# Separate gate and up weights in the FFN, and an earlier split of the latent key weights, in a two-layer float32 trunk

## What is computed

```python
def layer_norm(x, g, b):
    ...
    y = (xf - mu) * lax.rsqrt(var + LN_EPS) * g + b

def swiglu(h, w_gate, w_up, w_down):
    return (jax.nn.silu(h @ w_gate) * (h @ w_up)) @ w_down

def mla_project(h, pos, w_dq, g_q, w_uq, w_dkv, g_kv, w_uk):
    c_q = rms_norm(h @ w_dq, g_q)          # w_dq: 1024 x 512
    ...
    kv = h @ w_dkv                         # w_dkv: 1024 x 320
    ...

for i in range(DEPTH):                     # 0: pool mixer, 1: latent attention
    ...
    hp = layer_norm(ALPHA * hp + mix_p, ln_g[i, 0], ln_b[i, 0])
    hp = layer_norm(ALPHA * hp + swiglu(hp, ffn_w_gate[i], ffn_w_up[i], ffn_w_down[i]), ln_g[i, 1], ln_b[i, 1])
    # and the same for the sample rows hs
```

## Time and profile before

| | us |
|---|---|
| median of 3 runs | 2572.41 |
| lowest, highest | 2571.08, 2573.94 |
| profiled execution | 2571.08 |
| its span, first to last instruction | 2569.3 |

### The profile page before, as it was taken

The page is one execution under the profiler, slowest core; times in us unless marked ns, Lnnn a source line. Parts: engine busy times, 40 slices in busy tenths (PEclk is TensorE's granted clock), DMA queues, the critical chain, the costliest instruction groups (busy, mean ns, idle before and its releaser), DMA issues.

```text
span 2569.3 us, 35922 instructions
## 1 busy us (share of the span) xinstructions
PE 2463.7 (96%) x13347; PEld 2120.0 (83%) x13347; DVE 1080.4 (42%) x1967; ACT 544.8 (21%) x945; POOL 639.3 (25%) x388
## 2 busy tenths in 40 slices
PE   8899999999999969999999999978999999999996
PEld 8799999999999858577777774448999999999995
DVE  4343444344434562434444454432344434443446
ACT  3311111111111253233223223433111111111112
POOL 3422222222222430111111100242222222222225
PEclk9999999999999989999999999989999999999998
DMA  5201111111111020100000003411111111111111
GB/s 174 58 25 49 49 38 35 49 49 39 35 49 49 29 61 16 36 16 17 17 17 17 9 9 100 148 49 50 49 49 34 39 49 49 35 38 49 49 33 70
DMA packets 132443, 117.84 MB, mean 46 GB/s; under 512 B 8896, under 2 KB 119448, under 8 KB 132352
## 3 DMA queue, kind: packets, MB, share of 16 engines
q1 hardware_dynamic: 132368, 116.83, 14.7%
HBM read 110.94 MB, written 6.42 MB: 46 GB/s over the span
## 4 chain that ended last, share of the span: by engine, by line
PE 92%; DVE 4%; issue 2%; ACT 1%; POOL 0%; DMA 0%; SPq 0%; ACTq 0%; DVEq 0%
PE ps L647 22%; PE ps L646 22%; PE ps L648 21%; PE ps L926 4%; PE ps L992 3%; PE ps L896 2%; PE ps L979 1%; PE ps L868 1%; PE ps L910 1%; PE ps L1076 1%; PE ps L901 1%; PE ps L716 1%; PE ps L1051 1%; PE ps L942 1%; PE ps L664 1%
## 5 line engine op out<-in xcount | busy, mean ns | idle before, releaser
L646 PE MATMUL ps<-XH,WGH 128*128 128x368 f32 x2112 | 699.4, 331 | 17.6 <-POOL WGL L1794 13.6
L647 PE MATMUL ps<-XL,WGH 128*128 128x368 f32 x2112 | 699.6, 331 | 0.0
L648 PE MATMUL ps<-XH,WGL 128*128 128x368 f32 x2112 | 697.1, 330 | 0.0
L1551 DVE TENSOR_TENSOR XR<-XR,ps 128x512 f32<-128x512 f32 x756 | 510.3, 685 | 8.8 <-PE ps L648 4.5
L1534 DVE TENSOR_TENSOR HF<-SG,ps 128x368 f32<-128x368 f32 x132 | 70.9, 537 | 939.9 <-PE ps L648 934.1
L646 PEld LDWEIGHTS ps<-XH,WGH 128*128 128x128 f32 x2112 | 398.5, 189 | 22.3 <-issue 18.9
L647 PEld LDWEIGHTS ps<-XL,WGH 128*128 128x128 f32 x2112 | 397.8, 188 | 1.9
L648 PEld LDWEIGHTS ps<-XH,WGL 128*128 128x128 f32 x2112 | 398.0, 188 | 0.0
L1785 POOL TENSOR_TENSOR HL<-HF,HH 128x368 fp32r<-128x368 f32 x132 | 129.7, 983 | 852.5 <-DVE HH L1538 852.5
L646 PE MATMUL ps<-WDH,HH 128*128 128x512 f32 (+1 forms) x792 | 311.7, 394 | 5.6 <-DVE XR L1551 5.6
L648 PE MATMUL ps<-WDH,HL 128*128 128x512 f32 (+1 forms) x792 | 314.2, 397 | 0.0
(11 more groups left out here) (208 smaller groups left out, 2737.7 us busy)
## 6 DMA issues: line engine op xcount, KB each, us to landing
RAWG<-ffn_w_gate SPq DMA_DIRECT2D x44, 512.0 KB, 5.5
RAWG<-ffn_w_up SPq DMA_DIRECT2D x44, 512.0 KB, 6.8
RAWD<-ffn_w_down SPq DMA_DIRECT2D x44, 512.0 KB, 3.4
CR<-cache_mla_l SPq DMA_DIRECT2D x64, 160.0 KB, 2.6
XR<-x_prompt SPq DMA_DIRECT2D x8, 512.0 KB, 12.0
WOP<-mla_w_o SPq DMA_DIRECT2D x8, 512.0 KB, 3.3
WOA<-mla_w_o SPq DMA_DIRECT2D x1, 4096.0 KB, 17.4
o_y_prompt<-XR SPq DMA_DIRECT2D x8, 512.0 KB, 2.6
```

The lines of the kernel that those rows point to most:

```text
L646: pe.matmul(out, w[0], x[0], start=start, stop=False)
L647: pe.matmul(out, w[0], x[1], start=False, stop=False)
L648: return pe.matmul(out, w[1], x[0], start=False, stop=stop)
L1551: dve.tensor_tensor(XR[0:r, t, ds], XR[0:r, t, ds], ps[0:r, 4 + 2 * w + half, :], ALU.add).then_inc(s_row[2 * l + 1], 1)
```

## The change

**Gate and up apart, in both layers.** `load_gate_up`, `split_gate_up` and `gate_up_low` get an index m (0 gate, 1 up) and handle half of RAWG, WGH and WGL each. There is one load semaphore for each half; f_ghi and f_glo count halves. ScalarE's gate half waits for the chunk's gate products (f_gmm), its up half for the up products. ScalarE does the gate half between the second and the third SiLU of a chunk and the up half behind the third; GpSimd does both halves between the second and the third HL. TensorE waits in the first unit of a chunk for the gate half ahead of the gate matmuls and for the up half ahead of the up matmuls. SP issues chunk 1's gate and up loads ahead of its wait for the first norm's gain and bias.

**Latent key weights.** All of w_dkv is loaded at once into WKRAW, which is the memory of WKL, after the down load of chunk 1 in layer 0. ScalarE copies it to WKH, and DVE subtracts in place to WKL, both behind the third chunk (n = 2), when the down sums of chunk 1 are done. For that, turn 0 of the loops on ScalarE and DVE is written out for layer 0. The pieces of w_dq stay where they were, as the only two.

```diff
-LATENT_HIGH = (0, 3, 7, 10)
-LATENT_LOW = (1, 4, 8, 11)
+LATENT_HIGH = (7, 10)
+LATENT_LOW = (8, 11)
...
+        WKRAW = place("WKRAW", [P, DC, ROW], F32, FFN_END + DC * ROW * 4)
...
             def ffn_loads(l):
-                load_gate_up(l, 0)
+                load_gate_up(l, 0, 0)
+                load_gate_up(l, 0, 1)
                 load_down(l, 0)
+                for m in (0, 1):
+                    sp.wait_ge(f_glo[l], m + 1)
+                    load_gate_up(l, 1, m)
                 gain_bias_used(2 * l)
                 load_gain_bias(sp, 2 * l + 1)
-                with sp.Fori(1, NF) as n:
-                    sp.wait_ge(f_glo[l], n)
-                    load_gate_up(l, n)
+                sp.wait_ge(f_dlo[l], 1)
+                load_down(l, 1)
+                if l == 0:
+                    sp.wait_ge(s_pool, NT)
+                    sp.wait_ge(s_cast, 3)
+                    sp.dma_start(WKRAW[:], a["mla_w_dkv"][0].rearrange("(c p) n -> p c n", p=P)).then_inc(m_wl, 16)
+                with sp.Fori(2, NF) as n:
+                    sp.wait_ge(f_glo[l], 2 * n - 1)
+                    load_gate_up(l, n, 0)
+                    sp.wait_ge(f_glo[l], 2 * n)
+                    load_gate_up(l, n, 1)
                     sp.wait_ge(f_dlo[l], n)
                     load_down(l, n)
...
                 for m, done in ((0, f_gmm[l]), (1, f_umm[l])):
+                    if j == 0:
+                        pe.wait_ge(f_glo[l], 2 * n + m + 1)
                     for c in range(DC):
...
-            def split_gate_up(l, n):
-                act.wait_ge(f_raw[l], 32 * (n + 1))
-                act.wait_ge(f_umm[l], 3 * n)
-                act.wait_ge(f_glo[l], n)
-                copy(WGH[:], RAWG[:]).then_inc(f_ghi[l], 1)
+            def split_gate_up(l, n, m):
+                act.wait_ge(f_raw[l][m], 16 * (n + 1))
+                if not (isinstance(n, int) and n == 0):
+                    act.wait_ge((f_gmm, f_umm)[m][l], 3 * n)
+                    act.wait_ge(f_glo[l], 2 * n - 1 + m)
+                copy(WGH[:, m], RAWG[:, m]).then_inc(f_ghi[l], 1)
...
+            def silu_and_split(l, n, even):
+                silu_unit(l, n, even, 0)
+                silu_unit(l, n, even, 1)
+                split_gate_up(l, n + 1, 0)
+                silu_unit(l, n, even, 2)
+                split_gate_up(l, n + 1, 1)
...
+                    silu_and_split(l, 2, True)
+                    split_down(l, 2)
+                    act.wait_ge(m_wl, 16)
+                    copy(WKH[:], WKRAW[:]).then_inc(m_whi, 1)
...
-                with act.Fori(0, (NF - 2) // 2) as i:
+                with act.Fori(1 - l, (NF - 2) // 2) as i:
...
+                    dve.wait_ge(m_whi, 1)
+                    dve.tensor_tensor(WKL[:], WKRAW[:], WKH[:].bitcast(F32), ALU.subtract).then_inc(m_wlo, 1)
+                with dve.Fori(1 - l, (NF - 2) // 2) as i:
...
-            def gate_up_low(l, n):
-                pool.wait_ge(f_ghi[l], n + 1)
-                pool.tensor_tensor(WGL[:], RAWG[:], WGH[:].bitcast(F32), ALU.subtract).then_inc(f_glo[l], 1)
+            def gate_up_low(l, n, m):
+                pool.wait_ge(f_ghi[l], 2 * n + m + 1)
+                pool.tensor_tensor(WGL[:, m], RAWG[:, m], WGH[:, m].bitcast(F32), ALU.subtract).then_inc(f_glo[l], 1)
+
+            def hidden_and_gate_up_low(l, n, even):
+                hidden_low_unit(l, n, even, 0)
+                hidden_low_unit(l, n, even, 1)
+                gate_up_low(l, n + 1, 0)
+                gate_up_low(l, n + 1, 1)
+                hidden_low_unit(l, n, even, 2)
```

More of the change, by code:

```diff
@@ L222, in hybrid_trunk @@
         s_y = sem("s_y")
-        f_raw, f_rawd = [sem(f"f_raw{l}") for l in (0, 1)], [sem(f"f_rawd{l}") for l in (0, 1)]
+        f_raw = [[sem(f"f_raw{l}_{m}") for m in (0, 1)] for l in (0, 1)]
+        f_rawd = [sem(f"f_rawd{l}") for l in (0, 1)]
         f_ghi, f_glo = [sem(f"f_ghi{l}") for l in (0, 1)], [sem(f"f_glo{l}") for l in (0, 1)]
@@ L522, in gain_bias_used, with load_gate_up @@
                     wait_normed(sp, k, ln_vector(k)[-1])
-            def load_gate_up(l, n):
-                for j, w in enumerate(("ffn_w_gate", "ffn_w_up")):
-                    sp.dma_start(RAWG[:, j], a[w][l].rearrange("(c p) f -> p c f", p=P)[:, :, bass.ds(n * P, P)]
-                                 ).then_inc(f_raw[l], 16)
+            def load_gate_up(l, n, m):
+                w = ("ffn_w_gate", "ffn_w_up")[m]
+                sp.dma_start(RAWG[:, m], a[w][l].rearrange("(c p) f -> p c f", p=P)[:, :, bass.ds(n * P, P)]
+                             ).then_inc(f_raw[l][m], 16)
             def load_down(l, n):
@@ L543, in _ @@
             ffn_loads(0)
-            for j, (w, width) in enumerate(LATENT_W):
+            for j in (0, 1):
                 if j == 0:
-                    sp.wait_ge(f_glo[0], NF)
+                    sp.wait_ge(f_glo[0], 2 * NF)
                 else:
-                    sp.wait_ge(m_wlo, j)
-                dst = RAWG[:].rearrange("p a b c -> p (a b c)")[:, 0:4 * width].rearrange("p (c n) -> p c n", c=4)
-                src = a[w][0].rearrange("(c p) n -> p c n", p=P)[:, 4 * (j % 2):4 * (j % 2) + 4, :]
+                    sp.wait_ge(m_wlo, 2)
+                dst = RAWG[:].rearrange("p a b c -> p (a b c)").rearrange("p (c n) -> p c n", c=4)
+                src = a["mla_w_dq"][0].rearrange("(c p) n -> p c n", p=P)[:, 4 * j:4 * j + 4, :]
                 sp.dma_start(dst, src).then_inc(m_wl, 16)
-            sp.wait_ge(m_wlo, len(LATENT_W))
+            sp.wait_ge(m_wlo, 3)
             for c in range(QC):
@@ L1180, in _ @@
                 if t == 2:
-                    split_gate_up(0, 0)
+                    split_gate_up(0, 0, 0)
+                    split_gate_up(0, 0, 1)
             for t in range(NT, NT + LN_LAG[0]):
@@ L1185, in latent_high @@
             def latent_high(j):
-                act.wait_ge(m_wl, 16 * (j + 1))
-                if j == 2:
+                act.wait_ge(m_wl, 16 * (j + 2))
+                if j == 0:
                     act.wait_ge(f_umm[0], 3 * NF)
-                width = LATENT_W[j][1]
-                dst = (WKH if j < 2 else WQH)[:, 4 * (j % 2):4 * (j % 2) + 4, :]
-                copy(dst, RAWG[:].rearrange("p a b c -> p (a b c)")[:, 0:4 * width].rearrange("p (c n) -> p c n", c=4)
-                     ).then_inc(m_whi, 1)
+                copy(WQH[:, 4 * j:4 * j + 4, :], RAWG[:].rearrange("p a b c -> p (a b c)").rearrange(
+                    "p (c n) -> p c n", c=4)).then_inc(m_whi, 1)
             def silu_unit(l, n, even, j):
@@ L1516, in latent_low @@
             def latent_low(j):
-                dve.wait_ge(m_whi, j + 1)
-                part = slice(4 * (j % 2), 4 * (j % 2) + 4)
-                hi, lo = (WKH, WKL) if j < 2 else (WQH, WQL)
-                dve.tensor_tensor(lo[:, part, :],
-                                  RAWG[:].rearrange("p a b c -> p (a b c)")[:, 0:4 * LATENT_W[j][1]].rearrange(
-                                      "p (c n) -> p c n", c=4),
-                                  hi[:, part, :].bitcast(F32), ALU.subtract).then_inc(m_wlo, 1)
+                dve.wait_ge(m_whi, j + 2)
+                part = slice(4 * j, 4 * j + 4)
+                dve.tensor_tensor(WQL[:, part, :],
+                                  RAWG[:].rearrange("p a b c -> p (a b c)").rearrange("p (c n) -> p c n", c=4),
+                                  WQH[:, part, :].bitcast(F32), ALU.subtract).then_inc(m_wlo, 1)
             def hidden_unit(l, n, even, j):
@@ L1556, in swiglu @@
                 dve.wait_ge(s_xr, NT * (2 * l + 1))
-                with dve.Fori(0, (NF - 2) // 2) as i:
+                if l == 0:
+                    hidden(l, 1, False)
+                    for t in range(NT):
+                        down_add(l, 0, True, t)
+                    hidden(l, 2, True)
+                    for t in range(NT):
+                        down_add(l, 1, False, t)
+                    dve.wait_ge(m_whi, 1)
+                    dve.tensor_tensor(WKL[:], WKRAW[:], WKH[:].bitcast(F32), ALU.subtract).then_inc(m_wlo, 1)
+                with dve.Fori(1 - l, (NF - 2) // 2) as i:
                     hidden(l, 2 * i + 1, False)
@@ L1819, in _ @@
             ln_pool(0, (0, 1, 2))
-            gate_up_low(0, 0)
+            gate_up_low(0, 0, 0)
+            gate_up_low(0, 0, 1)
             ln_pool(0, range(3, NT))
@@ L1867, in _ @@
             ln_pool(2, range(NT - 1))
-            gate_up_low(1, 0)
+            gate_up_low(1, 0, 0)
+            gate_up_low(1, 0, 1)
             ln_pool(2, (NT - 1,))
```

44 lines of the change are left out of this document (18 added, 26 removed).

## The result

The changed kernel takes 2555.28 us (median of 4 runs, 2549.46 to 2556.5), beside 2572.72 us for the kernel before on the same chip (4 runs): a ratio of 0.9924, 95% interval 0.9912 to 0.9936. That is 17.4 us faster; 21.2 were forecast, so the time lies 4.1 us above the forecast of 2551.2 and inside its range. Five later runs gave 2553.28 us beside 2573.28, which is 20.0 us faster. The profiled execution took 2554.78 us with a span of 2553.0 (before: 2571.08 and 2569.3), so the two traces differ by 16.3 us.

A forecast was written before the change was run, and what follows sets the result against it. Bound by TensorE nearly everywhere, the weight hand-over at two places, and DVE at layer 0's FFN end. Savings of 17.7 + 3.5 = 21.2 us gave 2549.9 by the profile, 2551.2 us as median; range 2547.5 to 2556.

The forecast's parts named there:

- What bounds the kernel: TensorE nearly everywhere, the weight hand-over at two places, and DVE at the end of layer 0's FFN.
- Part 1: First-to-second FF chunk, both layers: splitting gate and up removes stops and slow clock, 18.0 us together, 17.7 after allowance.
- 0.3 us of allowance: Taken off the 18.0 us for the four half hand-overs together, since both halves just fit.
- the margin: At the hand-overs: 3.69 us of path per half under 4.03 us of cover from 24 matmuls.
- Part 2: End of layer 0's FFN: without the second WKL, DVE's sum of a down tile starts 3.5 us sooner.
- the stop before the down tile: End of layer 0's FFN: TensorE's stop of 4.81 us was to shrink to 1.3 us.
- the tail wasn't hidden: Rival: at layer 0's FFN end another chain ends as late as DVE's, part 2 gives nothing; 2554.7 us; chance 0.11.
- the hand-over wasn't too long: Rival: each of the four halves about 1 us late, 4 us come back; 2555 to 2556 us; chance 0.12.
- no middle chunk stopped: Rival: TensorE's new mid-unit wait stops it in all 42 later chunks; 2584.8 us at 0.8 us each; chance 0.03.
- the sum: Whole kernel: 17.7 + 3.5 = 21.2 us off the profiled 2571.08 gives 2549.9, as a median 2551.2 us.
- the three places: First-to-second chunk hand-overs in layers 0 and 1, 9.66 and 8.34 us, and layer 0's FFN end, 3.5 us.
- two first rivals: Hidden tail at layer 0's FFN end, 2554.7 us, chance 0.11; hand-over too long, 2555 to 2556 us, chance 0.12.

The follow-up runs named there:

- the kernel before with idle matmuls: Kernel before plus 14 idle matmuls, results unused, in two TensorE stops near the last samples' outputs and last output projection; 2571.05 us.
- SiLU-first: Changed kernel with ScalarE's third SiLU of a chunk put ahead of the gate split; 2552.75 us.
- part 2 alone: Kernel before with only the latent key weights split behind the third chunk of the first FFN; gate and up handed over together as before; 2572.89 us.
- part 1 alone: Changed kernel with gate and up halves split and handed over separately, but latent key weights left in the tail as before; 2555.35 us.
- the delay: Changed kernel with 16 idle matmuls ahead of layer 0's last chunk, putting what follows 3.6 us later; 2560.01 us.
- handed over together: Changed kernel with TensorE waiting for both halves of WGL before a chunk instead of the gate half alone; 2567.55 us.

## Why the prediction was right, and where it was short

- *What bounds the kernel* held: the gain came from the places named and no other. WGL is gone from the waits.
- *Part 1*: forecast 9.66 and 8.34 us, measured 9.66 and 8.34. The 0.3 us of allowance wasn't used, and the margin was thin as said: the gate half was done 0.2 us before its matmul.
- *Part 2*: forecast 3.5, measured 3.54; the stop before the down tile 1.26 (1.3). WKH took 2.33 us (2.35) and WKL 2.92 (at most 2.96), and no stop stood beside them.
- *The rivals* with their mechanisms did not come: the tail wasn't hidden (3.54 us), the hand-over wasn't too long (no stop), no middle chunk stopped (no WGL in the list).
- *The step that failed is the sum.* It takes 21.2 us from the profiled execution as if all that lies behind the three places cost the same afterwards. In the profiled execution it did not: 4.7 us of half clock at the samples' end, and 0.4 at the start. In the times 3.8 us are missing in the first group of runs and 1.2 in the second (17.4 and 20.0 of 21.2). I had priced the low clock behind the stops that went, and not looked at where else the kernel stands at low clock, though the profile showed it. The range held the first group's median of 2555.28 by luck in part: it lies where the two first rivals would have put it, and the upper end, 2556, was there for one of them; neither occurred.
- *One row was taken as fixed that wasn't*: DVE's XR of 3.46 us at 896.30. GpSimd had begun 0.02 us ahead of it. The same rule that I used for the sum behind it, in the Trainium skill, "SBUF — State Buffer", section "SBUF: two separate sides" (of a DVE instruction with two SBUF inputs and a GpSimd one, whichever starts first blocks the other for its whole length), fits this row: XR and GB are both in SBUF. The runs agree: 3.46 when DVE came second, 1.23 when first or after a wait. So 2.2 us there fall by chance in either kernel (of the profiles with 1.23, one is of the kernel before with idle matmuls).
- The SiLU-first profile lost at the samples' end what the kernel before lost; beside the changed kernel's trace it gains 4.7 us there. Without these the changed kernel's profiled execution would come to 2554.78 - 4.7 = 2550.1 us, beside the 2549.9 that the sum gives from the profiled execution of before.

What the loss at the samples' end goes with can be read one step further ahead, at the 16 matmuls of sample 6, the last but one, behind the stop of 4.61 us, by windows from their start to where the clock rises (before, changed, part 2 alone):

```profile
1680.57:1683.67 3.10, 3.10 (x8) 1.72 (x9) 0.72 (x2) 0.00 (x0) 3.02 (x3) 0.50 0.03 8
```

```profile
1667.76:1670.50 2.74, 2.74 (x7) 1.56 (x8) 0.72 (x2) 0.00 (x0) 2.66 (x2) 0.50 0.02 6
```

```profile
1679.01:1684.98 5.97, 5.97 (x14) 3.25 (x15) 0.73 (x2) 0.00 (x0) 5.81 (x4) 0.50 0.01 3
```

All eight profiles with that stop and without idle matmuls at the samples' end fall into place. Where the clock was at 0.50 for the first 3.10 to 3.12 us (before, part 1 alone, SiLU first), some 7 us were lost up to 1737 us; where it rose at 2.74 or 2.78 us (both profiles of the changed kernel), 12.0; where it rose at 5.94 to 5.99 us (part 2 alone, the delay, handed over together), 12.7 to 13.3. The SiLU-first kernel has part 2 and is in the first group, so part 2 as such is not what costs the 5 us.

What stays open: why the clock rises at one of these moments and not at another, and why some 0.35 us there go with 5 us behind it. That five of the six profiles with part 2, and neither of the two without it, rose at a costly moment may be chance; eight profiles are too few to tell.

## What to carry to other kernels

Price a removed wait by the distance of two instructions on either side, as here: the three places came out to 0.1 us. Then look at every stretch behind it where the granted clock is below 1.00; what such stretches cost can move by as much as a small gain, and a part whose gain shows in the trace (3.54 us) may show nothing in the time, as part 2 alone did in eleven runs. Gaps too short to be worth closing for themselves may be worth filling for the clock: 2550.6 to 2540.8 us here, 7.8 us of it, by the traces, at the short gaps.
